# Function sets and the order of the first loads in a two-layer hybrid block

## The reference

```
c_act, cc_act = silu(c), silu(c_ctx)              # two conditioning vectors of 1024
for i in range(2):
    mod_x, mod_c = c_act @ w_mod[i] + b_mod[i], cc_act @ w_mod[i] + b_mod[i]   # 1024 x 6144, six parts
    u = rms_norm(h) * (1 + mod[1]) + mod[0]       # "mix" norm: rsqrt of a mean of squares
    proj = u @ w_in[i]                            # 1024 x 2480
    ... differential attention (softmax, rms_norm of each head), a bidirectional state-space scan
        (softplus, exp of decays, silu gates, rms_norm), latent attention (rms_norm of the latents, softmax)
    h = h + mod[2] * (mix @ w_out[i])
    u = ada_norm(h)                               # "ffn" norm
    h = h + mod[5] * moe(u)                       # 16 experts, 2 of them for a token, silu(gate) * up
out = rms_norm(h)                                 # "final" norm
```

## Time and profile before

| what | us |
|---|---|
| median of 3 runs (lowest, highest) | 1548.59 (1543.71, 1556.0) |
| the profiled execution, its own time | 1555.77 |
| its span | 1553.8 |
| ACT busy in it | 318.0 |
| ACT_TABLE_LOAD, 55 of them, part of ACT's busy time | 70.6 |

### The profile page before, as it was taken

The page is one execution under the profiler, slowest core; times in us unless marked ns, Lnnn a source line. Parts: engine busy times, 40 slices in busy tenths (PEclk is TensorE's granted clock), DMA queues, the critical chain, the costliest instruction groups (busy, mean ns, idle before and its releaser), DMA issues.

```text
span 1553.8 us, 13940 instructions
## 1 busy us (share of the span) xinstructions
PE 1256.8 (81%) x5161; PEld 584.9 (38%) x5161; DVE 466.4 (30%) x1088; ACT 318.0 (20%) x606; POOL 113.5 (7%) x94
## 2 busy tenths in 40 slices
PE   3799888868999549999898299976798299788792
PEld 1353333336654213333232146523467133222231
DVE  1311544656632501111111521465552401000014
ACT  0411201225420411111110322202351211001002
POOL 0000121630000020000000200034000100000001
PEclk8899999985679769999999599985578699899995
DMA  8998109980010289999999310032001599999952
GB/s 322 371 348 299 54 0 398 420 318 1 1 71 0 109 288 368 382 383 381 381 421 350 121 47 8 1 116 100 0 1 60 198 363 375 396 397 389 423 205 88
DMA packets 88237, 347.83 MB, mean 224 GB/s; under 512 B 7958, under 2 KB 39659, under 8 KB 65643
## 3 DMA queue, kind: packets, MB, share of 16 engines
q1 hardware_dynamic: 66880, 308.68, 51.7%
q10 hardware_dynamic: 17835, 25.69, 5.0%
q0 software_dynamic: 3456, 12.58, 2.2%
HBM read 302.89 MB, written 44.04 MB: 223 GB/s over the span
## 4 chain that ended last, share of the span: by engine, by line
PE 62%; DMA 15%; DVE 12%; ACT 4%; issue 3%; ACTq 3%; POOL 1%; SPq 0%; POOLq 0%; DVEq 0%
PE ps L799 15%; PE ps L457 11%; DMA ring<-in_exp_w_up 8%; PE ps L820 7%; PE ps L724 6%; PE ps L466 5%; PE ps L400 4%; DMA arena<-in_exp_w_up 4%; PE ps L703 3%; PE ps L678 2%; PE ps L422 2%; PE ps L632 2%; DMA ring<-in_w_mod 1%; PE ps L620 1%; PE ps L734 1%
## 5 line engine op out<-in xcount | busy, mean ns | idle before, releaser
L799 PE MATMUL ps<-ring,arena 128*64 128x512 f32 x1024 | 235.8, 615 | 26.2 <-DMA ring<-in_exp_w_up 26.2
L400 PE MATMUL ps<-cst,arena 128*128 128x128 f32 (+1 forms) x594 | 117.5, 336 | 110.2 <-DMA arena<-slots 37.7
L457 PE MATMUL ps<-u,ring 128*128 128x512 f32 (+1 forms) x416 | 168.0, 564 | 11.5 <-ACT u L1520 7.8
L400 PEld LDWEIGHTS ps<-cst,arena 128*128 128x128 f32 (+1 forms) x594 | 82.4, 172 | 197.6 <-issue 74.2
L1408 DVE TENSOR_TENSOR arena<-arena,ps 128x256 f32<-128x256 f32 x44 | 26.8, 609 | 424.9 <-ACT arena L1642 424.9
L799 PEld LDWEIGHTS ps<-ring,arena 128*64 128x64 f32 x1024 | 72.7, 141 | 167.3 <-issue 139.5
L457 PEld LDWEIGHTS ps<-u,ring 128*128 128x128 f32 x416 | 80.0, 194 | 98.4 <-issue 93.3
L820 PE MATMUL ps<-arena 128*64 128x512 f32 x512 | 115.4, 592 | 0.9 <-ACT arena L1646 0.9
L799 PE MATMUL ps<-arena 128*64 128x512 f32 x384 | 90.8, 628 | 16.9 <-DMA arena<-in_exp_w_up 16.9
L724 PE MATMUL ps<-u,ring 128*128 128x512 f32 (+1 forms) x256 | 88.6, 511 | 1.0 <-DVE u L1252 1.0
L1642 ACT ACTIVATE arena<-ps 128x256 f32<-128x256 f32 x44 | 16.9, 384 | 335.7 <-PE ps L799 335.7
(11 more groups left out here) (250 smaller groups left out, 1234.5 us busy)
## 6 DMA issues: line engine op xcount, KB each, us to landing
ring<-in_w_mod SPq DMA_DIRECT2D x24, 2048.0 KB, 13.6
ring<-in_exp_w_gate SPq DMA_DIRECT2D x22, 2048.0 KB, 22.8
ring<-in_exp_w_up SPq DMA_DIRECT2D x22, 2048.0 KB, 27.8
arena<-in_exp_w_down SPq DMA_DIRECT2D x22, 2048.0 KB, 22.6
slots<-zeros SPq DMA_DIRECT2D x4, 6144.0 KB, 41.2
arena<-in_exp_w_gate SPq DMA_DIRECT2D x10, 2048.0 KB, 23.6
arena<-in_exp_w_up SPq DMA_DIRECT2D x10, 2048.0 KB, 29.2
u<-in_exp_w_down SPq DMA_DIRECT2D x10, 2048.0 KB, 24.7
```

Of the source, the lines that this page charges most:

```text
L400: return nc.tensor.transpose(dst, src, ident[0:n, 0:n])
L457: last = nc.tensor.matmul(bank[row:row + width, 0:T - c0], w[:, k, n:n + width], u[:, k, c0:T], start=(k == 0), stop=(k == KT - 1))
L799: last = nc.tensor.matmul(ps[BLOCK * half:BLOCK * half + BLOCK, 2 + b % 2, :].rearrange("p (s n) -> p s n", s=2), x_k, pair[:, :, a:a + 25 ...
```

## The change

It has three parts. (1) A helper `exp_and_ln()` loads the set `natural_log_exp_and_others` by hand: at the start, after the Silu instructions of the projection, after that of z, and after the experts; `silu_and_others` is loaded by hand ahead of the expert loop. (2) SP's queue begins with the identity and the two conditioning vectors (into 16 rows of `modrow`), then modulation chunk 0, tokens 0 and 1, chunk 1, tokens 2 and 3, chunk 2, chunk 3 and the rest; SP no longer waits for `const_landed`. PE turns the conditioning rows first, in a bank "conds" of their own; ACT's Exp reads it there. The five modulation parts stand between the token turns and the first norm (1, 1, 1 and 2 parts) instead of 2 and 3; the vector rows are turned after the tokens. (3) ACT issues `cst` without the identity and four vector loads, then the Exp of the conditioning vectors, then the other seven vector loads. Broadcasts, latent up-projections and router weights move to POOL's queue; DVE waits for the broadcasts in `take_steps` of layer 0 instead of ahead of the first norm.

```diff
@@ pe
-                pe.wait_ge(S("wu_landed"), 32 * (l + 1))
+                pe.wait_ge(S("wu_landed", l), 32)
...
+            def turn_tokens(t):
+                pe.wait_ge(S("tokens_landed", t), 16)
...
+            pe.wait_ge(S("cond_landed"), 48)
+            close_bank(tr(open_bank("conds")[:, 0:2 * KT], cond_rows))
+            pe.wait_ge(S("cond_ready"), 1)
+            spare(1)
+            turn_tokens(0)
+            turn_tokens(1)
+            spare(1)
+            turn_tokens(2)
+            turn_tokens(3)
+            spare(1)
             pe.wait_ge(S("const_landed"), 16 * (1 + n_vec_dmas))
             pe.wait_ge(S("ones_ready"), 2)
             bank = open_bank("vecs")
...
             for l in range(DEPTH):
-                if l == 0:
-                    pe.wait_ge(S("cond_ready"), 1)
-                    spare(2)
                 norm_mean(f"{l}mix", 0)
                 if l == 0:
-                    spare(3)
+                    spare(2)
@@ dve, norm and take_steps
                 if name == "0mix":
-                    spare(5)
+                    spare(4)
                 dve.wait_ge(S("rstd_ready"), NORMS.index(name) + 1)
                 for k in range(KT):
+                    if name == "0mix" and k == 2:
+                        spare(1)
                     tt(u[:, k, c0:T], h[:, k, c0:T], rstd[:, c0:T], ALU.mult).then_inc(S("u_scaled"), 1)
...
             def take_steps(l):
+                if l == 0:
+                    dve.wait_ge(S("bcast_landed"), 16 * n_bcast_dmas)
@@ dve, start: "conds" first, "vecs" after the squares
-            dve.wait_ge(S("bcast_landed"), 16 * n_bcast_dmas)
+            bank = claim("vecs")
...
@@ act
+            def exp_and_ln():
+                nc.scalar.preload_act_table_set("natural_log_exp_and_others")
...
                     a(xbc[:, m, c0:T], xbc[:, m, c0:T], ACT.Silu).then_inc(S("xbc_ready"), 1)
+                exp_and_ln()
...
                 a(z[:, FIRST_T[l]:TT, :], z[:, FIRST_T[l]:TT, :], ACT.Silu).then_inc(S("z_ready"), 1)
+                exp_and_ln()
...
+                nc.scalar.preload_act_table_set("silu_and_others")
                 blocks = expert_blocks(l)
...
                 act.sem_inc(S("all_stored", l), 1)
+                exp_and_ln()
                 act.wait_ge(S("gates_ready"), l + 1)
...
-            act.dma_start(cst[:, :], consts).then_inc(S("const_landed"), 16)
-            for dst, src in vec_loads:
+            exp_and_ln()
+            act.dma_start(cst[:, P:NCONST], consts[:, P:NCONST]).then_inc(S("const_landed"), 16)
+            for dst, src in vec_loads[:4]:
                 act.dma_start(dst, src).then_inc(S("const_landed"), 16)
+            act.wait_ge(filled, entry["conds"] + 1)
+            a(small[:, 32:48], ps[:, entry["conds"] % 2, 0:2 * KT], ACT.Exp, scale=-1.0).then_inc(S("cond_exp"), 1)
+            for dst, src in vec_loads[4:]:
+                act.dma_start(dst, src).then_inc(S("const_landed"), 16)
...
-            wait_evac("vecs")
-            a(small[:, 32:48], vec[:, 0, V_CCTX:V_CCTX + 16], ACT.Exp, scale=-1.0).then_inc(S("cond_exp"), 1)
-            for dst, src in bcast_loads:
-                act.dma_start(dst, src).then_inc(S("bcast_landed"), 16)
-            act.dma_start(rw[:, :, :], router_w.rearrange("(k p) e -> p k e", p=P)).then_inc(S("bcast_landed"), 16)
-            load_up(0)
@@ pool, start
+            for dst, src in bcast_loads:
+                g.dma_start(dst, src).then_inc(S("bcast_landed"), 16)
+            g.dma_start(wuq[:, :, :], mla_w_uq[0].rearrange("(k p) n -> p k n", p=P)).then_inc(S("wu_landed", 0), 16)
+            g.dma_start(wukv[:, :], mla_w_ukv[0]).then_inc(S("wu_landed", 0), 16)
+            g.dma_start(rw[:, :, :], router_w.rearrange("(k p) e -> p k e", p=P)).then_inc(S("bcast_landed"), 16)
@@ sp, start
-            for t in range(TT):
+            def load_tokens(t):
...
-            sp.wait_ge(S("const_landed"), 16 * (1 + n_vec_dmas))
+            sp.dma_start(ident, consts[:, 0:P]).then_inc(S("cond_landed"), 16)
+            for dst, src in cond_loads:
+                sp.dma_start(dst, src).then_inc(S("cond_landed"), 16)
             for key in chunks:
...
                 load(ring_at[key], key)
+                if ring_at[key] < 2:
+                    for t in range(2):
+                        load_tokens(2 * ring_at[key] + t)
```

More of the change, by code:

```diff
@@ L35 @@
 MLA_SCALE = HD ** -0.5
-V_BMOD, V_GMIX, V_GFFN, V_CONVW, V_CONVB, V_QG, V_KVG, V_SSDG, V_SUBG, V_FING, V_CCTX, V_C, NVEC = (
-    0, 48, 56, 64, 82, 88, 90, 91, 95, 96, 104, 112, 120)
+V_BMOD, V_GMIX, V_GFFN, V_CONVW, V_CONVB, V_QG, V_KVG, V_SSDG, V_SUBG, V_FING, NVEC = (
+    0, 48, 56, 64, 82, 88, 90, 91, 95, 96, 104)
 NVECS = (NVEC, V_FING)
@@ L363, in hybrid_dit_kernel @@
                               da_subln_g.rearrange("l (r p) -> r l p", r=1)))
-        for row, src in ((V_FING, final_norm_g), (V_CCTX, c_ctx), (V_C, c[0])):
-            vec_loads.append((vecrows[row:row + 8, 0, :], src.rearrange("(r p) -> r p", p=P)))
+        vec_loads.append((vecrows[V_FING:V_FING + 8, 0, :], final_norm_g.rearrange("(r p) -> r p", p=P)))
         for l in range(DEPTH):
@@ L371, in hybrid_dit_kernel @@
                 bcast_loads.append((bcast[:, l, at_b:at_b + n], src.partition_broadcast(P)))
+        cond_rows = modrow[0:2 * KT, 0:P]
+        cond_loads = [(cond_rows[KT * i:KT * i + KT, :], src.rearrange("(r p) -> r p", p=P))
+                      for i, src in enumerate((c_ctx, c[0]))]
         n_vec_dmas, n_bcast_dmas = len(vec_loads), len(bcast_loads) + 1
@@ L852, in _ @@
                 pe.sem_inc(S("down_done", l), len(expert_blocks(l)))
+            def turn_tokens(t):
+                pe.wait_ge(S("tokens_landed", t), 16)
+                for half in range(2):
+                    bank = open_bank(f"h{t}{half}")
+                    for m in range(4):
+                        last = tr(bank[:, P * m:P * m + P], tok[:, t, 512 * half + P * m:512 * half + P * m + P])
+                    close_bank(last)
+            pe.wait_ge(S("cond_landed"), 48)
[8 more added lines that the diff above has]
+            spare(1)
             pe.wait_ge(S("const_landed"), 16 * (1 + n_vec_dmas))
@@ L1428, in _ @@
             link(v.memset(cond[:, :, :], 0.0))
-            bank = claim("vecs")
-            for l in range(DEPTH):
-                last = v.tensor_copy(vec[:, l, 0:NVECS[l]], bank[:, P * l:P * l + NVECS[l]])
-            emptied(last)
-            own_read()
+            bank = claim("conds")[:, 0:2 * KT].rearrange("p (c k) -> p c k", c=2)
             dve.wait_ge(S("cond_exp"), 1)
@@ L1437, in _ @@
             link(v.reciprocal(small[:, 32:48], small[:, 32:48]))
-            tt(cond[:, :, 0:2].rearrange("p k c -> p c k"), vec[:, 0, V_CCTX:V_CCTX + 16].rearrange(
-                "p (c k) -> p c k", c=2), small[:, 32:48].rearrange("p (c k) -> p c k", c=2),
-               ALU.mult).then_inc(S("cond_ready"), 1)
+            emptied(tt(cond[:, :, 0:2].rearrange("p k c -> p c k"), bank,
+                       small[:, 32:48].rearrange("p (c k) -> p c k", c=2), ALU.mult))
+            own_read()
+            dve.sem_inc(S("cond_ready"), 1)
             for t in range(TT):
@@ L1446, in _ @@
                 add_square("0mix", 0, k)
-            dve.wait_ge(S("bcast_landed"), 16 * n_bcast_dmas)
+            bank = claim("vecs")
+            for l in range(DEPTH):
+                last = v.tensor_copy(vec[:, l, 0:NVECS[l]], bank[:, P * l:P * l + NVECS[l]])
+            emptied(last)
+            own_read()
             for l in range(DEPTH):
```

11 lines of the change are left out of this document (2 added, 9 removed).

## The result

| kernel | median (lowest, highest), us | runs |
|---|---|---|
| before | 1550.03 (1543.71, 1556.0) | 4 |
| changed | 1500.72 (1494.68, 1504.6) | 4 |

The ratio is 0.9671, with a 95% interval of 0.9642 to 0.9699: some 51 us less, where 29.8 were forecast. The direction was right, the size was not. The profiled execution took 1498.55 us, its span is 1496.4 (57.4 shorter than before), and its mean granted clock is 0.885 where it was 0.861.

What follows compares the result with a forecast made beforehand. No one engine bounds the whole; the start and ACT's chain in norms, scan and attention can gain. Start 12.1, scan 5.1, norms 5.1 and attention 7.5 make 29.8 us off 1548.6: forecast 1519, range 1500 to 1537.

Steps and rivals of the forecast that it cites:

- All other stages keep their length: Closing assumption of the sum: outside start, last scan tiles, norms and attention, nothing gets shorter or longer.
- the attention term: Six rsqrt in attention without table loads: 1.4 us each for five, 0.5 for the first, 7.5 us gained.
- a rival in which the clock falls: PE kept at its low clock level in attention and part of the output projection: 36 us slower, 1585; chance 0.05.
- The start: One stream of modulation, tokens and x weights: first projection at 42.5 us instead of 54.59, 12.1 us gained, at most 14.9.
- the eight squares ... are done by 30: First norm: tokens 2 and 3 land at about 24 us, squares need 4.27 us and finish before chunk 3.
- Last scan tile: End of each layer's scan: two table loads fewer on DVE's path, 2.57 us per layer, 5.1 us gained.
- Norms: Four norms (ffn twice, layer 1 mix, final) lose the load between Ln and Exp: 1.28 us each, 5.1 us.
- Expert entry: One 1.28 us load on PE's path per layer, priced 0 because the weight stream sets the end; at most 2.6.
- More comes back: Rival: all attention loads count (15.4), expert entries 2.6, start 14.9: 43 us gained, 1505; chance 0.14.
- Late constants: Rival: vector loads land after chunk 3 or the stream slows; start gains 3.6 to 8, total 1532; chance 0.17.
- sets that do not hold: Rival: table loads return beside Square, Identity or Copy, only the start gains, 12.1 us: 1536.5; chance 0.05.
- starved loads of POOL: Rival: POOL's loads wait until the zeros are stored, DVE and PE lose 20 us: gain 10, 1539; chance 0.03.

Runs made afterwards that it cites:

- e3: The changed kernel with two table loads put back ahead of each of the six rsqrt of attention: 1532.78 us, ratio 0.9871 to the kernel before.
- e5: The kernel before, table loads kept, with seven useless matmuls ahead of PE's wait at each of attention's six rsqrt: 1535.35 us, ratio 0.989.
- e4: The changed kernel with one table load put back ahead of each of the six rsqrt of attention: 1512.86 us, ratio 0.9746 to the kernel before.
- e6: The changed kernel with 17 useless 128x512 matmuls where PE waits at each attention's entry: 1508.84 us, ratio 0.9736 to the kernel before.
- e7: The changed kernel with all four token loads behind modulation chunk 0 and the parts of chunks 1 and 2 behind all token turns: 1494.15 us.
- e12: The changed kernel without the hand-placed Silu set ahead of the experts, so the loop keeps two loads per layer: 1507.02 us, ratio 0.9701.
- e11: e7 with POOL's loads of up-projections and router held back until the first norm's squares are summed: 1498.26 us, ratio 0.9641 to the kernel before.

## Why the prediction was partly right and mostly too small

**The step that failed** is in the sum, "All other stages keep their length", together with the attention term: the six rsqrt were priced as idle time of PE, 7.5 us, and the idle time did shrink by 6.3. What was left out is that PE's busy time is no constant: it fell by 21.9 us in attention on the same matmuls, and by another 2.7 in layer 0's output projection (57.91 to 55.20, clock 0.95 to 1.00) and 2.8 in layer 1's (30.67 at 0.91 to 27.89 at 1.00). These 27.4 us are the excess: on the profiled executions 57.4 us went, 27.6 more than forecast, and the other misses (start -5.4, attention's idle time -1.2, norms 1.8, entries 2.6, the rest 2.3) cancel. By the ratio the excess is some 21, since the profiled execution of before was a long one of its kernel. The prediction could have had it from its own rows: clocks of 0.63, 0.66 and 0.90 are mixtures of two levels, and I used them only for a rival in which the clock falls. I wrote that "less stalling is no reason for a lower clock" and didn't turn the sentence round. Two runs settle the cause: e3 brings the loads back and loses 32 us where ACT has only 15.4 of work more; e5 keeps the loads, fills the stalls with 22.4 us of useless matmuls and gains 17. e4, 12 us lost for 7.7 of loads, points the same way and is less clean.

The Trainium skill, "TensorE: Matmul & The Clock Gate", section "A second HAM failure mode: psum-queue depth-cycling", tells, for a bf16 kernel, of PE idling briefly and often between groups of matmuls, with the clock going up and down and each re-warming paid for. The rows at 388.52 and 418.57 of the kernel before show the like in float32, with 20 and 17 us at the low level behind waits of 2.39 and 1.79 us. That PE stays at 0.50 through 50.00 us of unbroken work (e6) is not what a story of idle time explains, and no run here says why.

**The start** was taken at 12.1 and gave 8.0, of which 6.7 outlived the first group: the x matmuls stood at the low level for longer than before, which cost 1.3. Of the 4.1 missing, 1.1 is the choice of 42.5 where the sum gave 43.6, and 1.2 is chunk 3. The stream was sized well (chunk 3 at 37.5 against 36.3, x at 43.7 against 42.2), and neither the late vector loads nor POOL's queue got in the way; POOL's broadcasts landed 5.9 to 9.4 us after issue. What failed was "the eight squares ... are done by 30": I had looked at when tokens 2 and 3 land and not at where their turns stand in PE's program, behind the part of a chunk that lands at 25. So the mean ran at 38.41, and the last part waited 2.4 us behind it. e7 takes just that away and gets 3.2 us in the trace.

**Last scan tile**: 2.56 per layer, forecast 2.57. **Norms**: three of the four gave 1.28, 1.28 and 1.27 us; that of layer 0's ffn gave 3.1 with the router. The other 1.8 are PE's clock again: the mean's matmul took 2.07 us before (clock of that stretch 0.50) and 1.13 after (0.74), and the first part of the router 7.65 us (0.62) and 6.74 (0.70). **Loads**: 13, as counted; their price was 1.283 us and no more. The Trainium skill, "ScalarE: Activation LUTs", section "What ACT_TABLE_LOAD costs", gives a drain of 1380 ns on top for every switch of set; two loads less shortened the last scan tile by 2.56 us, which leaves no room for it here.

**Expert entry**: forecast 0, because the stream behind it sets the end. The trace gives 0.95 and 1.65, and e12, which puts the loads back, is 6 us slower. The 1.28 us of the load on PE's path at the entry was not taken back by the stream. The "at most 2.6" was the right value by the trace; e12, expected to lose 2 to 3, lost more, and what the rest is was not followed.

**Rivals.** "More comes back" had its sign and its mixture of terms, but its 43 us came from all table-load time counting as idle time and from a start of 14.9; neither held. Only its 2.6 for the entries did. That its total is the nearest is a coincidence. Late constants, sets that do not hold and starved loads of POOL did not occur. The clock in attention moved by more than the 0.05 named as a sign of being wrong, upward: from 0.63 to 0.70 in layer 0 and from 0.66 to 0.81 in layer 1.

**Still open:** why the first part of attention is at 1.2 GHz in layer 0 of every kernel, and in layer 1 of all but those with fills at the entry, although PE is busy nearly all the time; how long a wait has to be for the clock to fall behind it, and why the clock came up and fell again in layer 0 but not in layer 1, in e4 with loads and in e11 without; how much of e11's gain at the start reaches the end.

## What to carry to other kernels

When PE's granted clock in a stage lies between 0.5 and 1.0, reckon that a stall in it may be worth more than its own length: look at what the clock does behind the stall, and add half of the low stretch (here 5 to 12 us for a wait of about 2). Whether one stall has such a stretch behind it can't be told from its length alone. Price an engine's busy time again at the clock of the stage after the edit, and ask it in both signs. And for a reordered start, follow each transfer through the program of the engine that takes it: a tile that has landed is no use while its turn stands behind a wait for a later chunk.

## What the runs showed of the hardware

- In the kernel before, e3 and e4, where PE's clock was up in attention, a wait of 1.66 to 2.75 us for ACT's copies had 10 to 24 us at 1.2 GHz with it, beginning between about a microsecond before its end and a microsecond behind it. Shorter waits are mixed: falls came with waits of 1.29 us (e11), 1.06 and 0.82 (e5, for DVE) and 0.67 (e4, at 404.99, 2.4 us behind), and none came with waits of 1.46 in e6's layer 1 (at 1090.58), of 0.93 in e4's (at 1126.54) or of 0.82 in the changed kernel (at 411.25).
- Useless matmuls in those waits raised the speed of the kernel: 22.4 us of work, 17 us gained (e5). The same at the entry of attention, with at least twice the work that the waits there could hold, cost 8 (e6), though layer 1's attention then ran at 1.00 throughout.
- An fp32 matmul call of 128x256 or 128x512 shows as two records: 42 calls in e5, 84 records of 426 ns.
- Ten small loads from POOL's queue landed in 5.9 to 9.4 us beside a full weight stream; behind four chunks, from ACT's queue, they had taken 8.7 to 21.7.
